# A hybrid encoder step on one core: routing the last tokens tile by tile ahead of the experts

## What is computed

```python
x = x + merged @ p["w_out"]
x = x + hierarchical_moe(rmsnorm(x, p["g_ffn"]), p)
...
def hierarchical_moe(h, p):
    lg = (h @ p["w_rg"]).astype(jnp.float32) + p["b_rg"].astype(jnp.float32)
    pg = jax.nn.softmax(lg, axis=-1)
    g_onehot = jax.nn.one_hot(jnp.argmax(lg, axis=-1), N_EXPERT_GROUPS, dtype=jnp.float32)
    ...
    le_sel = jnp.sum(le * g_onehot[..., None], axis=-2)
    tv, ti = lax.top_k(le_sel, TOP_K_IN_GROUP)
    ...
    for e in range(N_EXPERTS):
        hid = jax.nn.silu(h @ p["w_e1"][e]) * (h @ p["w_e3"][e])
        y = y + gate[..., e:e + 1] * (hid @ p["w_e2"][e])
```

## Time and profile before

| what | value |
|---|---|
| median of 3 runs | 673.11 us (672.87 to 674.49) |
| the profiled execution | 672.77 us |
| its span, first to last instruction | 671.0 us |
| TensorE matmul busy | 616.7 us (92% of the span) |
| TensorE weight loads busy | 381.5 us (57%) |
| VectorE busy | 329.3 us (49%) |
| ScalarE busy | 170.4 us (25%) |
| GpSimd busy | 151.8 us (23%) |
| moved by the DMA engines | 150.55 MB, mean 224 GB/s |
| mean granted clock of TensorE | 0.974 of full speed |

### The profile page before, as it was taken

How to read it: one execution, slowest core, us unless ns; L and a number is a source line. 1 busy time by engine, 2 the same in 40 slices (tenths; PEclk the granted TensorE clock), 3 DMA queues, 4 the chain that set the end, 5 groups by cost and what they waited for, 6 DMA issues and landing times.

```text
span 671.0 us, 9897 instructions
## 1 busy us (share of the span) xinstructions
PE 616.7 (92%) x3652; PEld 381.5 (57%) x3652; DVE 329.3 (49%) x864; ACT 170.4 (25%) x540; POOL 151.8 (23%) x341
## 2 busy tenths in 40 slices
PE   6999999999999889999999999989999999778863
PEld 4678876776545557676677756844444433333320
DVE  2163755978787988711133321474434524515132
ACT  4425224330558413222100101121222112010200
POOL 1497445833478943000000000000000000000000
PEclk8899999999999899999999999979999999999997
DMA  9863472212301073042289990087999999999972
GB/s 259 196 212 127 157 228 94 64 64 65 122 0 33 1 251 95 17 142 67 101 241 405 399 379 33 12 365 282 416 416 417 415 418 416 419 417 417 414 319 80
DMA packets 61377, 150.55 MB, mean 224 GB/s; under 512 B 12304, under 2 KB 40400, under 8 KB 53136
## 3 DMA queue, kind: packets, MB, share of 16 engines
q1 hardware_dynamic: 61328, 149.89, 60.4%
HBM read 147.12 MB, written 2.76 MB: 223 GB/s over the span
## 4 chain that ended last, share of the span: by engine, by line
PE 58%; DVE 5%; issue 3%; POOL 2%; ACT 1%; DVEq 0%
PE PS L802 18%; PE PS L1149 9%; PE PS L1074 7%; PE PS L1185 6%; PE PS L810 5%; PE PS L1175 4%; PE PS L1112 2%; PE PS L923 1%; PE PS L946 1%; PE PS L1051 1%; ACT xg L1480 1%; PE PS L1123 1%; DVE rotB L1655 1%; PE PS L931 1%; PE PS L863 1%
## 5 line engine op out<-in xcount | busy, mean ns | idle before, releaser
L802 PE MATMUL PS<-hT,W 128*128 128x320 f32 x448 | 128.7, 443 | 1.1 <-issue 1.1
L802 PEld LDWEIGHTS PS<-hT,W 128*128 128x128 f32 x448 | 85.3, 194 | 39.2 <-issue 6.3
L1149 PE MATMUL PS<-E,xT 128*32 128x256 f32 x1024 | 61.8, 395 | 15.3 <-issue 15.3
L1149 PEld LDWEIGHTS PS<-E,xT 128*32 128x32 f32 x1024 | 36.6, 114 | 45.1 <-issue 29.9
L2098 POOL TENSOR_SCALAR means<-sums 128x4 f32<-128x4 f32 (+3 forms) x35 | 8.0, 229 | 225.4 <-ACT junk L1282 224.0
L1074 PE MATMUL PS<-h,S 128*128 128x512 f32 (+1 forms) x96 | 48.9, 637 | 1.8 <-DVE S L1892 1.8
L810 PE MATMUL PS<-W,hT 128*128 128x256 f32 (+5 forms) x256 | 41.8, 353 | 1.6 <-ACT memT L1264 1.6
L1185 PE MATMUL PS<-yb,WG 128*128 128x512 f32 (+1 forms) x96 | 39.9, 618 | 0.9 <-DVE yb L2009 0.9
L2027 DVE TENSOR_TENSOR X<-X,PS 128x512 f32<-128x512 f32 (+1 forms) x48 | 32.9, 686 | 10.0 <-PE PS L1185 8.4
L810 PEld LDWEIGHTS PS<-W,hT 128*128 128x128 f32 (+1 forms) x256 | 31.5, 163 | 10.2 <-ACT memT L1264 1.8
L810 PE MATMUL PS<-W,mergedT 128*128 128x384 f32 (+3 forms) x192 | 35.8, 382 | 1.6 <-DVE mergedT L1805 1.6
(11 more groups left out here) (309 smaller groups left out, 964.8 us busy)
## 6 DMA issues: line engine op xcount, KB each, us to landing
E<-in_w_e SPq DMA_DIRECT2D x96, 1024.0 KB, 22.3
W<-in_w_in SPq DMA_DIRECT2D x7, 1536.0 KB, 7.3
W<-in_w_in SPq DMA_DIRECT2D x7, 1024.0 KB, 9.5
W<-in_w_mem_kv SPq DMA_DIRECT2D x4, 1024.0 KB, 6.2
W<-in_w_glu SPq DMA_DIRECT2D x4, 768.0 KB, 7.5
W<-in_w_out SPq DMA_DIRECT2D x2, 1536.0 KB, 14.9
X<-in_x_prompt SPq DMA_DIRECT2D x4, 512.0 KB, 5.7
W<-in_w_o_mem SPq DMA_DIRECT2D x1, 1536.0 KB, 6.3
```

The costliest lines, as they stand in the source:

```text
L802: ins = mm(out[:, 0:TOK], w[:, k, cols:cols + 128], rhs[:, k, :], start=(k == 0), stop=(k == kt - 1))
L1149: ins = mm(PS[r:r + B, 2 + par, 0:FF], xT[:, k, place_ + B * n:place_ + B * n + B], E13[slot][:, :, k, 128 * j:128 * j + 128], start=(k == ...
```

## The change

The routing is cut into one step for each tile instead of one for tiles 0 and 1 and one for tile 2, and four kinds of pieces move.

- `experts` is split in two. `in_group(ts)` holds lines 1845 to 1860, up to the two best experts inside the group; `experts(ts)` holds the rest, up to the one-hot rows. Each is called for one tile at a time, and a `residual` stands between the two halves for tiles 0 and 1.
- `homes` is called for each tile, with its own rank product. `first_ranks` now ranks tile 0 alone and stands behind the transposes of tile 1; the new `next_ranks` ranks tile 1 and starts the sums for tile 2, and stands behind the transposes of tile 2.
- Row selection (`choose_first`) is called for a tile and a half of the columns. Tile 0's first half stands ahead of the transposes of tile 2, its second half between `next_ranks` and the router product of tile 2; tile 1's two products follow the router; tile 2's two are last, as before. `normed(2)` is cut into two halves and moved from ahead of `logits(2)` to both sides of the last `homes`.
- `warming` is new: a product of the identity with columns of `h2`, written to a bank that nobody reads. There are four: 512 columns ahead of `last_ranks`, 512 and 256 behind it, and 256 behind the last selection.

```diff
             def first_ranks():
                 pe.wait_ge(s["onehot_ready"], 1)
                 pe.wait_ge(s["const_loaded"], 16)
-                mm(PS[:, YB, 0:2 * NE], const("upper"), both[:, 0:2, :].rearrange("p t e -> p (t e)"), start=True, stop=False)
+                mm(PS[:, YB, 0:NE], const("upper"), both[:, 0, :], start=True, stop=True).then_inc(s["rank_full"], 1)
+
+            def next_ranks():
+                pe.wait_ge(s["onehot_ready"], 2)
+                mm(PS[:, YB, NE:2 * NE], const("upper"), both[:, 1, :], start=True, stop=False)
                 mm(PS[:, YB, NE:2 * NE], const("ones"), both[:, 0, :], start=False, stop=True).then_inc(s["rank_full"], 1)
...
+            def warming(out, cols):
+                mm(PS[:, out, 0:cols], ident, h2[:, 0, 0:cols], start=True, stop=True)
...
-            def choose_first(tiles):
-                pe.wait_ge(s["chosen"], tiles[-1])
-                pe.wait_ge(s["h2_ready"], tiles[-1] + 1)
-                rows_done(FIRST_ROWS, tiles, s["rows_full"])
+            def choose_first(t, c):
+                pe.wait_ge(s["chosen"], t + 1)
+                pe.wait_ge(s["h2_ready"], t + 1 + (c if t == NT - 1 else 0))
+                ins = tile_rows(FIRST_ROWS, t, c)
+                if t == NT - 1:
+                    ins.then_inc(s["rows_full"], 1)
...
                 elif kind == "yT":
                     if which[0] == NT - 1:
+                        choose_first(0, 0)
+                    rows_turned(*which)
+                    if which[0] == 1:
                         first_ranks()
-                    rows_turned(*which)
+                    if which[0] == NT - 1:
+                        next_ranks()
+                        choose_first(0, 1)
                 else:
                     route(*which)
-            choose_first((0, 1))
+            spare = UNIT_NO[LAST_WOUT[NT - 1]] % RING
+            for c in range(2):
+                choose_first(1, c)
+            warming(spare, 512)
             last_ranks()
-            choose_first((2,))
+            warming(spare, 512)
+            warming(spare, 256)
+            for c in range(2):
+                choose_first(2, c)
+            warming(spare, 256)
...
             residual(1, 1)
             logits(0)
+            in_group(only[0])
             residual(2, 1)
+            experts(only[0])
             residual(2, 2)
             normed(1)
+            homes(only[0], PS[:, YB, 0:NE])
             residual(1, 2)
             logits(1)
-            experts(first)
+            in_group(only[1])
             residual(0, 2)
-            homes(first, 1, PS[:, YB, 0:2 * NE])
-            normed(2)
+            experts(only[1])
+            homes(only[1], PS[:, YB, NE:2 * NE])
             logits(2)
-            experts(last)
+            in_group(only[2])
+            experts(only[2])
...
             st.mark(V_.tensor_reduce(rs[:, 8, :], ex4[:, 1], AX.X, ALU.add))
-            homes(last, 2, PS[:, LAST_RANKS, 0:NE])
+            normed(2, slice(0, 512))
+            homes(only[2], PS[:, LAST_RANKS, 0:NE])
+            normed(2, slice(512, D))
```

38 lines of the change are left out of this document (19 added, 19 removed).

## The result

| | kernel before | changed kernel |
|---|---|---|
| median | 673.44 us (672.87 to 674.49, 4 runs) | 668.93 us (668.19 to 669.19, 4 runs) |
| profiled execution | 672.77 us | 669.19 us |
| its span | 671.0 us | 667.3 us |
| mean granted clock in it | 0.974 | 0.984 |

The ratio of the medians is 0.9929, with a 95% interval of 0.9912 to 0.9947: the kernel became 0.5 to 0.9% faster. The two profiled spans differ by 3.7 us, the medians by 4.5.

The account below looks back on a forecast made before the run. The weight transfer stream, started by the end of `up(0)`, was taken to bound the kernel. Gains of 0.7 + 2.8 = 3.5 us took the profiled 672.77 to 669.3, forecast as a 669.6 us median, range 668.8 to 672.2.

Parts of the forecast that it names:

- From the router to the last ranks: Tile 2's router to the last `homes`: ranks no longer held up, `homes` 0.7 us earlier (bounds 0.2 and 1.1).
- The clock term: From the transposes of collected rows to the end of `up(0)`: full clock gains 2.8 us, nothing if not full.
- The bound: Whole end of the run: one unbroken transfer stream sets it, `up(0)`'s end starts that stream; TensorE's later pace is swallowed.
- Up to the router of tile 2: From the last `wout` to tile 2's router: router starts 0.6 us later, 0.5 taken (bounds 0.2 and 0.9).
- The filler: Tile 0's two selection products ahead of tile 2's router, 1.0 us each; forecast cost: router 0.6 us later.
- The rival's argument: Against the clock still falling at the transposes (672.4 us, chance 0.09): 1280 warming columns in the waits around the last selection.
- After `up(0)`: Start of the expert loop: new TensorE wait of 3.6 us, clock falls in or behind it, without cost to the stream.
- The sum: Whole kernel: 0.7 + 2.8 = 3.5 us off the profiled execution, forecast 669.6 us.
- The clock did not fall at the transposes: Rival at the transposes of collected rows: clock still falls there, only 0.7 of 3.5 us comes, 672.4 us; chance 0.09.
- A slow last pair: Rival at the last expert pair: clock may fall in the wait before it, adding 1.35 us, 671.0 us; chance 0.10.
- The filler did not hold up tile 2: Rival ahead of tile 2's router: half clock makes early selections delay `homes` 2.7 us, slower at 675.8 us; chance 0.06.
- The stream did not run dry: Rival in the first expert pairs: `down(1)` comes too late for the stream, up to 2 us lost, 671.6 us; chance 0.04.

Follow-up runs that it names:

- e2: Changed kernel, but SP's first refill of w_e1 and w_e3 also waits for the first transposed hidden rows: 672.65 us, 0.9998 of before.
- e6: Changed kernel with seven more transposes of the hidden rows in each of the expert pairs 2 to 9: 668.97 us, 0.9951 of before.
- e5: Changed kernel with tile 0's two selection products moved behind tile 2's router, in place of the first warming product: 669.65 us, 0.9945 of before.
- e1: Changed kernel without its four warming products: 672.53 us, 0.9991 of before.
- e11: The kernel of e8 once more, unedited: 665.07 us, 0.9878 of before.
- e4: Kernel before plus warming alone, 512 and 256 columns behind the last ranks, 256 behind the last selection: 670.9 us, 0.9973 of before.
- e3: Changed kernel with each warming product replaced by 128 x 128 transposes (seven for 512 columns, three for 256): 670.66 us, 0.9961 of before.
- e7: Changed kernel with the first half of `normed(2)` moved ahead of tile 2's logits: 668.88 us, 0.9944 of before.
- e8: e7 plus two warming products of 512 columns ahead of the last pair's `up`: 664.8 us, 0.9905 of before.

## Why the prediction was right or wrong

The way and the mechanism came as forecast, and the gain was larger: 3.5 us were forecast and 4.5 measured. The range was laid against a kernel before of 673.11 us, and its lower end, 668.8, allows a gain of 4.3 from there. The step that failed is the term *From the router to the last ranks*, the gain up to the start of the last `homes`: 0.7 us with an upper bound of 1.1, measured 1.28. It was short because the step before it kept the router of tile 2 at its old 1.52 us of partly half clock, where it now took 1.12. The clock term was 0.4 us too large, and 0.8 us of the 4.5 lie outside the profiled pair, from where is open.

**The bound: right.** The end was set by the stream, the stream by the end of `up(0)`, and TensorE's later pace counted for nothing. The changed trace shows it (`up(0)` 3.74 us earlier, last pair 3.73), e2 and e6 show both sides, and the stream column holds within 0.2 us for all others.

**Up to the router of tile 2: wrong in its sum.** I forecast the router 0.6 us later and used 0.5. It started 0.35 us later (437.91 against 437.56), mostly since the last `wout` ended at 433.95 and not at 434.15. It ended no later at all: 5.08 us behind the last `wout`, against 5.15. The filler does cost what its products take (e5 without it: 4.10, so 0.98 us). What I left out is that the router itself had run partly at half clock, 1.52 us in the earlier trace rows, and at full clock takes 1.12: a saving of 0.4. I had the fall of the clock between 438 and 441 in front of me and used it for the chance of a rival, not for the length of the product that lay in it.

**From the router to the last ranks: mis-sized by that error.** The router's end was forecast at 439.6 and came at 439.03, and `homes` came 1.28 us earlier instead of 0.7. Every later step of this term came as worked out: the three wide products end before the one-hot rows are there (TensorE then waits 0.39 us), the half of `normed(2)` costs 0.66 us (442.58 to 443.24), and the selection starts 1.30 us earlier. So the term as a whole was short by the error of the step before it.

**The clock term: the mechanism right, the size a little too large.** Forecast 2.8 us (7.6 to 4.75), measured 2.44 (7.57 to 5.13). What is missing is an idle 0.33 us ahead of `up(0)`, a wait for ScalarE's copies to `xT` that was hidden at half clock, when the transposes lasted until the copies were done. In the rows of the loop from which I took the two lengths a `down` stands between them, and no such wait shows. e1 shows who earned the term: the warming products, and they earned 1.64 us more, since without them the clock would have fallen ahead of the selection in the new order. In my working the products only kept what the order had won; in fact the order without them has waits of 1.24 and 2.20 us and lost its own gain. The rival's argument also counted 1280 columns of warming in the two waits around the last selection; there are 768 and 256.

**After `up(0)`: right in what counts.** The transpose came at 455.93 instead of the 456.7 named, the new wait is 3.02 us instead of 3.6. I expected the clock to fall in or behind it, and in this execution it stayed at 1.00; it did fall in others, as in e2 and e11, and cost nothing, as worked out.

**The sum: too small.** 0.7 + 2.8 = 3.5 us was forecast, and 1.30 + 2.44 = 3.74 measured in the profiled pair. The remaining 0.8 us of the 4.5 between the medians are not in this pair: the profile of before lay 0.7 us under the median of its four runs, that of the changed kernel 0.3 above. I had added 0.34 us for the first, from three runs. The runs of before scatter with the mean clock: of the 14 beside e11 the six with 0.969 or less took 673.2 to 675.6 us and the eight with 0.974 or more 671.1 to 672.8, though beside e4 some at 0.969 took 672.1 to 672.6. Two things in the traces could do that. One is the fall ahead of the router, which in e4, alike up to there, came earlier than in the trace of before and cost 1.35 us more; no trace of a kernel with the new order has it. The other is a last `up` at half clock, which costs 1.5 to 1.7 us. A slow pair in the midst of the stream, like the 5.01 us of the earlier trace rows, is swallowed. There is one trace of before, so that the changed kernel has fewer of these is likely and not shown, and the source of the 0.8 us stays open.

**The rivals.** The clock did not fall at the transposes; between wide products it stayed full over them. A slow last pair did not come in this trace, and it did in three others (e3, e5, e7: 14.75 to 14.95 us instead of 13.26), so it costs 1.5 to 1.7 us when it comes; I had 1.35. Whether it comes and goes between executions of one kernel no pair of traces shows. The filler did not hold up tile 2, the slower side; its mild form, 1 us of delay at full clock, is what e5 shows. The stream did not run dry.

## What to carry to other kernels

Where a stream of transfers sets the end, look for the one product that starts it, and make that product and the few ahead of it quick; the rest may be slow. A product without a reader can be worth more than a better order when it stands in a wait ahead of such a product: here, in the new order, four of them brought 4.1 us, and the order that was meant to be the gain brought nothing without them. When a forecast uses a clock for one stretch, go through every row in the stretches at half clock and ask what each would be at full, and compare kernels stage by stage rather than by their spans, so that a difference at the very end, as with e11's branch, isn't put down to the edit.

## What the runs showed of the hardware that was not expected

- **A conditional branch that takes 0.5 or 3.8 us.** Over a loop body that is skipped, TensorE's first branch took 3.6 to 3.9 us in all traces but those of e8 and e11, where it took 460 and 503 ns, with the whole end of the program 3.3 us shorter; the four behind it took some 0.22 us each in the traces of both kinds. The Trainium skill, page "Advanced Engine Details and Errata", section "Control Flow Timing", gives some 108 ns for a compare-and-branch; all five are above it.
- **The clock fell with waits of 1 us and less between products.** Before, it fell behind waits of 1.03 and 0.47 us with narrow ranks and 64-row transposes between them. In the loop, behind wide products, it stayed full through a wait of 3.07 us and was at half behind one of 3.05. So the length of a wait alone does not tell whether the clock falls.
- **The moment of the fall moves by itself.** Between before and e4, whose TensorE work is alike up to there, it came 1.1 us earlier in e4, counted from the last `wout`, and router and selection took 7.8 us together instead of 6.4.
- **A wait hidden by a slow engine comes up when it is quick.** The 0.33 us for the copies to `xT` stands in every trace in which the transposes ran at full clock, and in none in which they were slow.
